# A two-block layer on one core: small f32 matmuls in column groups, a forget bias as one row per head, a GpSimd product with one tensor operand

## The reference

```python
def first_block(x, ...):                       # norm, mixers, out projection, gated FFN
    z, xbc, dt_raw, q, kc, vc, ks, vs, kw, vw, gate_raw = split(rmsnorm(x) @ w_in)
    y_ssd = ssd_mixer(z, xbc, dt_raw, ...)     # conv, then ssd_chunked over 2 chunks of 128
    y_att = nsa_mixer(q, kc, vc, ks, vs, kw, vw, gate_raw, ...)
    h = x + concatenate([y_ssd, y_att]) @ w_out
    return rmsnorm(h + (silu(v @ w_gate) * (v @ w_up)) @ w_down)

# ssd_chunked: 16 heads of 64, state 128, 2 groups
y_diag = einsum('bclsgh,bcsghp->bclghp', cb[..., None] * decay, x)   # the mixer's values

# nsa_mixer: 16 heads of 64 on 4 key heads; 15 compressed keys; two full branches, gated
s_cmp = einsum('bshgd,bihd->bhgsi', q_grp, k_cmp) * scale            # the compressed scores
o = g[..., 0, :] * o_cmp + g[..., 1, :] * o_sel + g[..., 2, :] * o_win

def second_block(x, ...):
    # hgrn2_mixer: 8 heads of 128, gated recurrence over the sequence
    o_t = S_t^T q_t,  S_t = diag(f_t) S_{t-1} + k_t^T i_t
    # fox_mixer: 8 heads of 128
    cum = cumsum(log_sigmoid(f_logit), axis=1)
    s = einsum('bhqd,bhkd->bhqk', q_blk, kh) + c_blk[..., None] - cum[:, :, None, :]   # the forget bias
    p = softmax(where(causal, s, -inf))
    # then up projections, merge, w_o, norm, gated FFN (2 x 5632), norm
```

## Time and profile before

| | |
|---|---|
| time, median of 3 runs | 2577.07 us (2575.7 to 2577.09) |
| the profiled execution | 2574.19 us |
| its span, first to last instruction | 2572.2 us |
| TensorE busy | 2554.1 us, 13330 matmul records |
| weight loads (overlap the matmuls) | 2145.3 us |
| VectorE, ScalarE, GpSimd busy | 1523.9, 1245.4, 31.1 us |
| mean traffic | 200 GB/s |

### The profile page before, as it was taken

The page is one execution under the profiler, slowest core; times in us unless marked ns, Lnnn a source line. Parts: engine busy times, 40 slices in busy tenths (PEclk is TensorE's granted clock), DMA queues, the critical chain, the costliest instruction groups (busy, mean ns, idle before and its releaser), DMA issues.

```text
span 2572.2 us, 32831 instructions
## 1 busy us (share of the span) xinstructions
PE 2554.1 (99%) x13330; PEld 2145.3 (83%) x13330; DVE 1523.9 (59%) x1847; ACT 1245.4 (48%) x1573; POOL 31.1 (1%) x28
## 2 busy tenths in 40 slices
PE   9999999999999999999999999999999999999998
PEld 9977888888888888899888888888888888888887
DVE  6787776555555545576578554566655545555555
ACT  5565645444344434466455454534544444443443
POOL 0021000000000000000000000000000000000000
PEclk9999999999999999999999999999999999999999
DMA  8644557776667667676655556676576667766664
GB/s 303 181 139 124 163 153 257 215 220 211 194 215 220 209 193 211 213 230 217 191 173 166 164 152 201 183 258 213 180 227 215 222 191 210 216 220 194 210 208 147
DMA packets 172838, 515.01 MB, mean 200 GB/s; under 512 B 17104, under 2 KB 48080, under 8 KB 171632
## 3 DMA queue, kind: packets, MB, share of 16 engines
q1 hardware_dynamic: 172544, 512.77, 64.1%
q10 hardware_dynamic: 144, 0.15, 0.0%
HBM read 492.54 MB, written 19.92 MB: 199 GB/s over the span
## 4 chain that ended last, share of the span: by engine, by line
PE 96%; DVE 2%; ACT 1%; issue 0%; DMA 0%; SPq 0%; DVEq 0%; ACTq 0%
PE ps L507 95%; PE ps L511 1%; DVE W L1691 1%; DVE wlo L1691 1%; ACT W L1136 0%; ACT whi L1136 0%; DMA raw<-in_w_in 0%; DVE W L2189 0%; ACT L1136 0%; DVE W L2363 0%; ACT scr L1136 0%; DVE W L1694 0%; DVE h L1694 0%; DVE sm L1691 0%; DVE scr L1691 0%
## 5 line engine op out<-in xcount | busy, mean ns | idle before, releaser
L1691 DVE TENSOR_TENSOR wlo<-raw,whi 128x1024 fp32r<-128x1024 f32 x884 | 1084.6, 1230 | 953.5 <-ACT whi L1136 948.8
L1136 ACT ACTIVATE whi<-raw 128x1024 fp32r<-128x1024 f32 x884 | 933.8, 1058 | 1098.1 <-PE ps L507 1087.1
L507 PE MATMUL ps<-whi,xx 128*128 128x512 f32 x4160 | 1285.6, 390 | 0.0
L507 PEld LDWEIGHTS ps<-whi,xx 128*128 128x128 f32 x4160 | 778.1, 188 | 160.6 <-issue 0.5
L507 PE MATMUL ps<-wlo,xx 128*128 128x512 f32 x2080 | 809.5, 389 | 0.0
L507 PEld LDWEIGHTS ps<-wlo,xx 128*128 128x128 f32 x2080 | 390.4, 188 | 81.6
L507 PE MATMUL ps<-whi,hlo 128*128 128x512 f32 x944 | 368.5, 390 | 0.0
L507 PE MATMUL ps<-wlo,hhi 128*128 128x512 f32 x944 | 367.4, 389 | 0.0
L507 PE MATMUL ps<-whi,hhi 128*128 128x512 f32 x944 | 367.3, 389 | 0.0
L507 PE MATMUL ps<-xx,whi 128*128 128x256 f32 (+1 forms) x1344 | 323.3, 334 | 0.3 <-DVE xx L1694 0.3
L507 PE MATMUL ps<-xx,wlo 128*128 128x256 f32 x960 | 221.3, 280 | 0.1
(11 more groups left out here) (163 smaller groups left out, 904.3 us busy)
## 6 DMA issues: line engine op xcount, KB each, us to landing
raw<-in_gu SPq DMA_DIRECT2D x352, 512.0 KB, 4.3
raw<-in_w_in SPq DMA_DIRECT2D x256, 512.0 KB, 4.1
raw<-in_dn SPq DMA_DIRECT2D x176, 512.0 KB, 4.2
raw<-in_w_out SPq DMA_DIRECT2D x32, 512.0 KB, 3.7
raw<-in_w_up SPq DMA_DIRECT2D x32, 512.0 KB, 4.3
raw<-in_w_o SPq DMA_DIRECT2D x32, 512.0 KB, 4.1
W<-blocks SPq DMA_DIRECT2D x120, 128.0 KB, 2.7
blocks<-W SPq DMA_DIRECT2D x20, 512.0 KB, 6.4
```

Source lines behind the costliest of these rows:

```text
L507: return e.matmul(o, l, r, start=start, stop=stop, skip_group_check=skip)
L1136: return e.activation(o, i, f, **kw)
L1691: return e.tensor_tensor(o, a, b, op)
```

## The change

Six edits:

1. **Mixer values** (`ssd`). Each f32 matmul with 128x128 weights `MM` is cut into four with 32 weight columns, each writing its own 32 PSUM partitions.
2. **Compressed scores.** Likewise: the queries (64 rows by 128) are cut into four groups of 32 columns, for both row halves.
3. **Level 64 of the recurrence.** The two chunks write partitions 0 to 63 and 64 to 127 of one bank instead of two banks, and alternate.
4. **Forget bias.** TensorE makes, by three f32 matmuls with 16 weight columns, the running sums of all heads' log gates (rows 0 to 7 and again 8 to 15, 256 columns). ScalarE rounds them to fp32r (`fhi`), VectorE makes `frow`: the rounded sums in rows 0 to 7, the rests in rows 8 to 15. The bias of a head is then one fp32r matmul of 16 rows: the column -1 of the head's two rows (`fsel`), repeated 128 times, by `frow`. Only -cum of the key is added; what depends on the query alone drops out of the softmax. `prep`, `LU2` and the products on VectorE go. The tasks start two units later.
5. **GpSimd with one operand.** The gate product leaves VectorE; GpSimd multiplies each head's probabilities by two per-partition scalars (reciprocal, gate): 2 or 4 instructions per task instead of one with two tensors.
6. **Order.** `flatten` handles both key heads in one instruction (4 per step, twice as long). The compressed branch starts one step later and its transposes and values one more; the softplus of the mixer waits 35 units instead of 24.

```diff
-                for i in range(11):
+                for i in range(12):
...
-                                for par in range(2):
-                                    p0, g = par * 64, 2 * g2 + par
-                                    m = mm(pbs[par][:, (4 * g2 + r) * 15:(4 * g2 + r) * 15 + 15], qf[p0:p0 + 64, g2 * 4 + r, tb * 128:tb * 128 + 128],
-                                           kcT[p0:p0 + 64, g * 15:g * 15 + 15])
+                                for c0 in range(0, 128, 32):
+                                    for par in range(2):
+                                        p0, g, q0 = par * 64, 2 * g2 + par, tb * 128 + c0
+                                        m = mm(pbs[par][c0:c0 + 32, (4 * g2 + r) * 15:(4 * g2 + r) * 15 + 15], qf[p0:p0 + 64, g2 * 4 + r, q0:q0 + 32],
+                                               kcT[p0:p0 + 64, g * 15:g * 15 + 15])
...
-                            m = mm(pb[:, (4 * hq + r) * 64:(4 * hq + r) * 64 + 64], MM[:, j % 2, r, :], xd[:, c, hd * 64:hd * 64 + 64])
+                            for p0 in range(0, 128, 32):
+                                m = mm(pb[p0:p0 + 32, (4 * hq + r) * 64:(4 * hq + r) * 64 + 64], MM[:, j % 2, r, p0:p0 + 32], xd[:, c, hd * 64:hd * 64 + 64])
...
-                            for c in range(2):
-                                for r in range(4):
+                            for r in range(4):
+                                for c in range(2):
...
-                                        m = mm(pbs[c][0:64, r * 128 + 64:r * 128 + 128], kl[:, r, t:t + 64], ql[:, r, t + 64:t + 128])
+                                        m = mm(pbs[0][c * 64:c * 64 + 64, r * 64:r * 64 + 64], kl[:, r, t:t + 64], ql[:, r, t + 64:t + 128])
...
+                pb = take("fb")
+                on.wait_ge(s_lf, 1)
+                mm(pb[0:16, 0:128], lf2[:, 0, :], C("U"))
+                mm(pb[0:16, 128:256], lf2[:, 0, :], ones, stop=False)
+                mm(pb[0:16, 128:256], lf2[:, 1, :], C("U"), start=False).then_inc(s_fb, 1)
+                give("fb", when=(s_fr, 1))
+                yield
+                yield
                 yield
...
-                        if tb:
-                            mm(o[:, 0:128], LU[:, 1, r, :], SU, start=False, stop=False)
-                        m = mm(o, LU[:, 0, r, :], C("OS")[:, 256 - Kn:256], start=False, stop=True)
+                        m = mm(o, fsel[:, h0 + r:h0 + r + 1].to_broadcast([16, 128]), frow[:, 0:Kn], start=False, stop=True)
...
-            side = chain(begin(att, 7), both(att, compressed()), attention_T(), ssd())
+            side = chain(begin(att, 8), both(att, compressed()), attention_T(), ssd())
...
-                yield from later(24)
+                yield from later(35)
                 yield from softplus(1, 32, 1)
...
                             for q in range(2):
-                                for hq in range(2):
-                                    src = ckv[p0:p0 + 64, kv * 2 + hq, :].rearrange("p (i j) -> p i j", j=16)
...
+                                o = flat[jp * 64:jp * 64 + 64, kv, 8 * q:8 * q + 8, :].rearrange("p j (h r i) -> p h r j i", h=2, r=2)[:, :, par]
+                                i_ = src[:, :, q:q + 15, jp:16:2].rearrange("p h i j -> p h j i")
...
-                        on.wait_ge(s_gs, 1)
-                        own.up(e.reciprocal(z, z))
-                        mine()
-                        tt(z, z, att_gates(j), MUL).then_inc(s_w, 1)
+                        e.reciprocal(z, z).then_inc(s_w, 1)
...
+                on.wait_ge(s_fb, 1)
+                act(fhi, B("fb")[0:16, 0:256]).then_inc(s_fh, 1)
...
-                prep(0)
-                yield
-                yield from attend("a2", [(128 * (t[0] + 1), t[2]) for t in T2], N1, 1.0, foxw[0:2], fin, prep)
+                on.wait_ge(s_fb, 1)
+                mine()
+                e.tensor_copy(fsel, C("sel", 16)[:, 0:8])
+                yield
+                on.wait_ge(s_fh, 1)
+                stt(frow, fhi.bitcast(F), C("sel", 16)[:, 8:9], B("fb")[0:16, 0:256], MUL, ADD).then_inc(s_fr, 1)
+                yield
+                yield
+                yield from attend("a2", [(128 * (t[0] + 1), t[2]) for t in T2], N1, 1.0, foxw[0:2], fin)
...
         def gpsimd(e):
+            on.wait_ge(s_gs, 1)
...
-                e.tensor_tensor(p, p, bc(zsum[:, j, 0:nh], 2, [P, nh, 512 // nh]), MUL).then_inc(s_wp, 1)
+                for r in range(nh):
+                    p = PM1[j % 4][:, r * Kn:r * Kn + Kn]
+                    m = e.tensor_scalar(p, p, zsum[:, j, r:r + 1], att_gates(j)[:, r:r + 1], MUL, MUL)
+                m.then_inc(s_wp, 1)
```

More of the change, by code:

```diff
@@ L294, in build @@
         bv_ = W_(6144, 2, 1024)
-        LU2 = [W_(S0 + 8192 + 1024 * i, 2, 4, 128) for i in range(2)]
+        fsel, fhi, frow = (spare[0:16, 0, 0, x:x + n] for x, n in ((0, 8), (256, 256), (512, 256)))
         foxw = [W_(S0 + 10240 + 512 * i, 512) for i in range(6)]
@@ L326, in build @@
         lf = small(2, 8)
+        lf2 = small(2, 16)
+        f2 = lf2.rearrange("p a (c b) -> p a c b", c=2)
         d32 = dt.rearrange("p a b -> p (a b)")
@@ L855, in compressed @@
                             give("vb", gp, when=(s_bd, gp + 1))
-                    if i in (8, 9):
-                        tb = i - 8
+                    if i in (9, 10):
+                        tb = i - 9
                         for gp in range(2):
@@ L865, in compressed @@
                             give("co", tb, gp, when=(s_crd, 2 * tb + gp + 1))
-                    if i in (6, 7):
-                        tb = i - 6
+                    if i in (7, 8):
+                        tb = i - 7
                         pb = take("ct", tb)
@@ L993, in hgrn @@
                             on.wait_ge(s_scan, 8)
-                            pbs = [take("lev", hg, li, c) for c in range(2 if m_ == 64 else 1)]
-                            for c in range(2):
-                                for r in range(4):
+                            pbs = [take("lev", hg, li, 0)]
+                            for r in range(4):
+                                for c in range(2):
                                     t = c * 128
                                     if m_ == 64:
-                                        m = mm(pbs[c][0:64, r * 128 + 64:r * 128 + 128], kl[:, r, t:t + 64], ql[:, r, t + 64:t + 128])
+                                        m = mm(pbs[0][c * 64:c * 64 + 64, r * 64:r * 64 + 64], kl[:, r, t:t + 64], ql[:, r, t + 64:t + 128])
                                         continue
@@ L1038, in scores @@
                     Kn = 128 * (tb + 1)
-                    LU = LU2[j % 2]
-                    on.wait_ge(s_lu, j + 1)
+                    on.wait_ge(s_fr, 1)
                     for r in range(nh):
@@ L1443, in compressed @@
                         m.then_inc(s_ca, 1)
-                    if i in (7, 8):
-                        tb = i - 7
+                    if i in (8, 9):
+                        tb = i - 8
                         on.wait_ge(s_ct, tb + 1)
@@ L2103, in forget_gates @@
                 yield from softplus(2, l16, 16, True)
-                stt(l16, l16, 0.0, sp[3][:, 0:16], MIN, SUB).then_inc(s_lf, 1)
+                for d in range(2):
+                    m = stt(f2[:, :, d, :], lf, 0.0, two(sp[3][:, 0:16]), MIN, SUB)
+                m.then_inc(s_lf, 1)
             def rope(src, rot, dst, wait, ntile, landed):
@@ L2155, in taps, with attend @@
                     yield
-            def attend(lab, tasks, base, sc, SX, fin, prep=None):
+            def attend(lab, tasks, base, sc, SX, fin):
                 n = len(tasks)
@@ L2173, in attend @@
                         fin(i - 6)
-                    if prep is not None and i + 1 < n:
-                        prep(i + 1)
                     yield
@@ L2241, in compressed @@
                         tt(s, s, bc(mx16, 2, [P, 16, 15]), SUB).then_inc(s_cx, 1)
-                    if i in (9, 10):
-                        tb = i - 9
+                    if i in (10, 11):
+                        tb = i - 10
                         for gp in range(2):
@@ L2733, in constants @@
     put("join8", (np.arange(16)[:, None] % 8 == np.arange(8)[None, :]).astype(f))
+    p16 = np.arange(16)[:, None]
+    put("sel", np.concatenate([-(p16 % 8 == np.arange(8)[None, :]).astype(f), -(p16 >= 8).astype(f)], 1))
     put("cos", ct)
```

28 lines of the change are left out of this document (9 added, 19 removed).

## The result

The kernel after takes 2585.75 us (median, 2585.67 to 2585.99) beside 2576.57 (2575.38 to 2577.09) for the kernel before on the same chip: a ratio of 1.0038, 95% interval 1.0026 to 1.0050, some 9 us slower. The forecast was 2565, 12 us faster. The profiled execution has a span of 2584.0 us at a granted clock of 0.999, as that of the kernel before has, so the clock is no part of the loss.

A forecast was written before the change was run, and what follows sets the result against it. TensorE, busy 99% of the span, was taken as the bound: 7.9 us off its work plus 4.5 off its waits, 12.4 us from the median 2577.07, gave 2565 us; 8-in-10 range 2558 to 2573.

The forecast's parts named there:

- mixer values: Mixer's value matmuls in 32-column groups: 0.62 instead of 0.81 us a part, 8 parts, 1.5 us saved; bounds 0 and 3.0.
- compressed scores: Compressed branch's score matmuls, twice: 1.41 instead of 1.89 us at 0.011 per record, 1.0 us saved; bounds 0 and 2.4.
- level 64: Recurrence's level 64, twice 1.08 us: alternating between two column groups can halve it, 1.0 us saved; bounds 0 and 1.0.
- forget bias: Attention's bias as one fp32r matmul per head: 4.2 plus 0.9 saved, 0.74 for new sums, net 4.4 us.
- waits: TensorE's waits in the first block's attention stretch: 7.2 of 8.0 us attacked, 4.5 counted as saved.
- the analogue: Bias matmuls: no entry cost counted, since 64-column fp32r matmuls alternate freely with 128-column ones; 2.6 us kept as bound.
- the small tiles pay each time: Rival: bias matmuls cost 2.6 us more and value groups save nothing, 8.3 us gained, 2569; chance 0.09.
- after 235 us: Sign of being right: the softplus's two table loads on ScalarE, 1.28 us each, come after 235 us.
- no wait behind them: Sign of being right: TensorE has no wait behind the two moved table loads.
- no gap over 1 us: Sign of being right: TensorE shows no gap over 1 us before the score matmuls between 150 and 185 us.
- GpSimd turns the bound: Rival: longer GpSimd tasks block VectorE, deciding from 1.7 us a task; 2589 us at 2.3; chance 0.05.
- 0.24 us a task: GpSimd's one-operand task at 0.8 instead of 1.04 us blocks VectorE 0.24 less, 24 times, 5.8 us.

The follow-up runs named there:

- experiment five: The kernel after with 55 unused columns more, so that the constant table grows by 256 bytes a partition: 2566.83 us, ratio 0.9968.
- experiment eight: The kernel after with 55 unused columns and the bias matmuls on 128 rows instead of 16, the added rows zero: 2560.92 us, ratio 0.9946.
- experiment ten: The kernel of experiment eight with GpSimd's two-operand product and VectorE's product of sums and gates as in the kernel before: 2563.41 us, ratio 0.9951.
- experiment eleven: The kernel of experiment eight with the first softplus 11 units earlier again, inside the attention tasks: 2564.06 us, ratio 0.9952.
- Experiment six: The kernel before with 64 unused columns (256 bytes a partition) at the end of the constant table: 2576.03 us, ratio 1.0003.
- nine: The kernel of experiment five with the forget bias made as in the kernel before: 2565.36 us, ratio 0.9958.
- experiments three and four: The kernel before with 64-byte unused tensors ahead of and behind xx, or ahead of whi and behind wlo: 2629.9 and 2631.77 us.

## Why the prediction was wrong, and where it was right

The step that failed is the silent one. The forecast summed the parts that the diff adds, removes and moves and took every other instruction to cost what it did, while `("sel", 9)` moves the tensors behind the table. That is 18.4 us by the pace and 18.9 by experiment five beside the kernel after (2585.75 less 2566.83), twice what the rest of the change gains. No rival named it. The Trainium skill (SBUF — State Buffer, Operand start alignment) lets an operand start at any multiple of its element size and says that this is "about legality, not speed"; the runs agree that 32 bytes off is allowed, and show that in this form a distance off a multiple of 256 bytes costs 5 to 7 ns a matmul.

Without that shift the change gives 2566.83, inside the forecast's own range of 2561 to 2567, at its slow end. That is in part luck: by the traces the change gains 7.0 us and not 12.4, the bias lost instead of gaining, and some 2 us come from the base of the sum, the median, in which the clock of the kernel before has often fallen (below). The terms, from the timelines (from the start of the last weight matmul ahead of a burst to the start of the second one behind it, so that a longer entry and exit count):

| term | forecast | measured | how |
|---|---|---|---|
| mixer values | -1.5 | -0.9 | 8 by 0.114 |
| compressed scores | -1.0 | -1.4 | 2 by 0.70 |
| level 64 | -1.0 | -0.9 | 2 by 0.46 |
| forget bias | -4.4 | +1.5 | 2 by +0.89, 4 by -0.30, sums +0.96 |
| waits | -4.5 | -5.3 | 8.8 to 3.5 |
| sum | -12.4 | -7.0 | spans 2572.2 and 2565.3: -6.9 |

**Values.** Forecast were 0.54 us for the sets and 0.08 more to enter; measured are 0.59, the exit to the next weight matmul included, and 0.09. Eight parts make the small miss 0.6. **Compressed scores.** 0.009 us a record instead of the 0.011 taken, so the saving lies between the value taken and the upper bound. **Level 64.** 0.46 us each instead of 0.5, near its bound.

**Forget bias.** The step that failed was the analogue: 16 fp32r matmuls of 64 weight columns that alternate with 128 ones free of charge were taken to stand for tiles of 16 rows. They don't. A change of height costs in fp32r as well, and both neighbours pay, 0.32 us a head and not the 0.16 of the bound. In experiment eight, with the height (and the copy that fills the zero rows) as the only difference, the term is 4.2 us, near the 4.4 of the forecast. The rival "the small tiles pay each time" had the mechanism and half of its price. The trace of before had the warning unread: four records of 16 rows and 8 columns (start us, us):

```profile
1473.50 0.39 PE L507 MATMUL ps<-wlo,xx 128*128 128x512 f32 x1
1473.82 0.61 PE L507 MATMUL ps<-cst,thin 16*128 16x8 f32 x4
1474.36 0.73 PE L507 MATMUL ps<-whi,xx 128*128 128x512 f32 x2
```
They start 0.32 us after the last weight matmul, for 0.23, and take 0.54, 0.13 each for 8 columns, where a record of full height and 128 columns takes 0.11. The Trainium skill (TensorEngine Tiling, Key Properties) says that a change of the tiling mode drains the engine; the forecast set the fp32r rows against it. The cost of the 16-row matmuls agrees with it, though no run shows what the engine does at the change; those of 64 columns still don't.

The sums were forecast at 0.74 and cost 0.96 (1.64 from 1485.83 to 1487.47, for the 0.68 of three plain weight matmuls). The log gates were not late, as forecast.

**Waits.** Nearly right, and two of the causes are now shown: the one-operand form on GpSimd, which takes the gate product off VectorE, is worth 2.5 us (experiment ten), the moved table loads 3.1 (experiment eleven). In both a part is the clock, which the forecast didn't count: a wait can cost more than its length. The third, the transpose that comes one unit later, was not undone on its own; its 1.2 us of wait are gone from the trace. In a stretch like that of the earlier trace rows, VectorE is no longer full (us, busy, PEclk, DMA share, GB/s):

```profile
134.53:145.08 10.55, 9.75 (x24) 1.00 0.45 131
```
The table loads stand at 247.47 and 251.81 in the timeline of ScalarE, "after 235 us" as forecast.
But the matmuls that read the compressed probabilities, near 254, now wait 0.5 us for ScalarE, the new `ACT W` row above, so "no wait behind them" was not quite right. Nor was "no gap over 1 us" between 150 and 185: one of 1.05 us is left near 180.

**GpSimd.** Its price was wrong, and so was the mechanism by which it was to act; the direction of the effect was right. Two undisturbed tasks, and between them two tasks beside a busy VectorE:

```profile
129.99 1.75 POOL L2600 TENSOR_SCALAR W<-W,sm 128x128 f32<-128x128 f32 x4 [0.71 <-DVE sm L2207]
...
134.53 7.00 POOL L2600 TENSOR_SCALAR W<-W,sm 128x128 f32<-128x128 f32 x8 [2.79 <-DVE sm L2207]
...
161.41 1.10 POOL L2600 TENSOR_SCALAR scr<-scr,sm 128x256 f32<-128x256 f32 x2 [3.27 <-DVE sm L2207]
```
A task takes 1.75 us in four pieces and 1.10 in two, for 1.04 in one; 0.8 was forecast. (Two sizes give an estimate: 0.33 us for each instruction and 0.11 for 128 columns.) Beside VectorE it takes 3.5 us, and the mean over the 24 tasks is 2.1 us (50.7 us of the page) against 1.3 before. The rival "GpSimd turns the bound" was to decide from 1.7 us a task, and it didn't. What failed in it, and in the forecast's 0.24 us a task, is the same step: both charged GpSimd's time to VectorE. One flattening step on VectorE while GpSimd works, first in experiment eight (one operand), then in experiment ten (two):

```profile
138.78 2.13 DVE L1704 TENSOR_TENSOR W<-W,cst 64x240 f32<-64x240 f32 x4
139.87 2.87 DVE L1704 TENSOR_TENSOR W<-W,cst 64x240 f32<-64x240 f32 x4
```
The weight splits of VectorE from 112 to 250 us take 1.25 us on the mean in experiment eight and 1.37 in ten, for 1.22 far from attention. So the two-operand product held VectorE up, by some 0.7 us a step, and the one-operand form, though longer, hardly does: it is GpSimd that is stretched. A flattening step went from 3.11 to 2.13 us; the instructions of twice the size account for the first 0.24 (3.11 to 2.87, forecast 0.4), GpSimd's other form for the rest.

The profiled execution of before took 2574.19 us, the low end of its runs (2573.9 to 2577.2 over the study). By profiled spans experiment five gains 6.9 us, by medians 9.15. The 2 us between them are the clock, as far as the traces tell. Experiment six is the kernel before with an unused pad; its profiled execution is 1.8 us longer (span 2574.0) and loses 1.5 of them behind the 2.45 us wait, at a granted clock of 0.50. Nearly all runs of the kernel before above 2576 us show a mean granted clock of 0.998, those below it 0.999, while the kernels without the long waits (after, five, eight, nine) agree within 0.6 us.

## What to carry to other kernels

A diff that changes the size of an early allocation can change the pace of every matmul whose two operands lie on either side of it: compare the distance from moving to stationary operand modulo 256 bytes before and after, and look in the trace at matmuls that the diff doesn't touch. A pad of unused columns up to the next multiple of 256 bytes cost nothing here (experiment six) and is the first control to run. A 16-row fp32r operand between full tiles was better padded to the full height than multiplied as it is. A wait of TensorE of some 2 us can cost more than its length: read the granted clock behind it.

## What the runs showed of the hardware

- The 512-column f32 matmuls with 128 by 128 weights ran at 0.227 us start to start with the two operands 0 modulo 256 bytes apart in SBUF, and at 0.232 to 0.233 at 32, 64 and 128; moving all of them by 64 bytes together changed nothing. What in the chip does this was not found. Other distances, and other widths, were not tried on their own; in experiments three and four, the other way about (`xx` streaming, `whi` as weights, 256 and 512 columns), the group's mean went from 334 to 332 ns with the distance off by 64, and its 512-column matmuls from 233 to between 229 and 230 ns start to start, so a multiple of 256 is not the best for every form.
- An fp32r matmul of 16 rows between f32 matmuls of 128 rows costs 0.32 us a head more than the same sum on 128 rows (0.64 and 0.88 us a head against 0.32 and 0.55).
- Column groups of 32 with 15 moving columns, rows halved as well, issue a record each 0.009 us (1.19 over 128).
- Behind waits of TensorE of 1.73 us (experiment ten) and 2.45 us (experiments six and eleven) the granted clock was 0.50 over the 3 us of the windows shown, which cost 1.5 to 1.6 us each; behind waits as long in the profiled execution of the kernel before it stayed at 1.00.
- GpSimd's two-operand product beside VectorE made a flattening step 2.87 us long instead of 2.13 beside the one-operand form; the one-operand form itself went from 1.75 to 3.5 us a task.
